# Redistributing a gather pass's rows over VectorE's stages, and the gate stage ahead of the output product, in a two-block transformer on one core

## The reference, cut to what matters

```python
def peer_ffn(x, w_q, sub_keys, u, v):      # 8 heads, top-16 of 16384 experts each: 128 rows per token
    ...
    expert_idx = jnp.take_along_axis(cand_i, top_pos, axis=-1)
    gates = jax.nn.softmax(top_s, axis=-1)
    ub = jnp.take(u, eb, axis=0)
    act = jax.nn.gelu(jnp.einsum('thkd,td->thk', ub, xb), approximate=False)
    vb = jnp.take(v, eb, axis=0)
    return jnp.einsum('thk,thkd->td', gb * act, vb)

# first_block, end of a layer: x = x + sigmoid(x @ ple_w_gate[i]) * (p[i] @ ple_w_proj[i])
# second_block: h = rms_norm_2(x); z = h @ w_in
#   x = x + concatenate([y_nsa, y_conv, y_gla]) @ w_out
#   x = x + (silu(h @ ffn_w_gate) * (h @ ffn_w_up)) @ ffn_w_down
```

## Time and profile before

| | us |
|---|---|
| median of 3 runs | 2252.76 |
| lowest, highest | 2241.89, 2260.28 |
| span of the profiled execution | 2259.6 |
| VectorE, TensorE, POOL busy in it | 1450.5, 1527.2, 985.0 |
| DMA, mean over the span | 337 GB/s |

### The profile page before, as it was taken

One profiled execution on the slowest core, in us unless ns is written; L12 is line 12 of the kernel. 1 busy time (PEld: TensorE's weight loads), 2 busy tenths in 40 slices (PEclk: granted clock), 3 DMA queues, 4 the chain that ended last, 5 costly groups with the idle time before them and its releaser, 6 DMA issues. The chain is left out here.

```text
span 2259.6 us, 17114 instructions
## 1 busy us (share of the span) xinstructions
PE 1527.2 (68%) x5282; PEld 879.4 (39%) x5282; DVE 1450.5 (64%) x3168; ACT 323.1 (14%) x778; POOL 985.0 (44%) x1058
## 2 busy tenths in 40 slices
PE   8987600467656539776573897666576656899998
PEld 7446600222225225422341552235252232376453
DVE  1236898779587875678688468786978676444101
ACT  1220100011112111111120111111321000123111
POOL 0102466667665555566455456653446444000000
PEclk9989855688867669987766899778767877899999
DMA  7436999999999999999999999999989999973672
GB/s 260 85 117 245 394 408 409 337 360 370 371 379 403 404 406 358 361 365 367 407 399 405 365 342 368 375 401 386 391 293 403 399 398 399 366 243 130 242 260 93
DMA packets 268005, 760.62 MB, mean 337 GB/s; under 512 B 21295, under 2 KB 46590, under 8 KB 267275
## 3 DMA queue, kind: packets, MB, share of 16 engines
q0 software_dynamic: 147456, 536.94, 61.8%
q1 hardware_dynamic: 120458, 222.60, 27.8%
HBM read 756.84 MB, written 2.62 MB: 336 GB/s over the span
## 5 line engine op out<-in xcount | busy, mean ns | idle before, releaser
L946 POOL DMA_INDIRECT ROWS<-in_peer_u,IDX x512 | 483.3, 944 | 455.5 <-DVE ROWS L991 266.9
L946 POOL DMA_INDIRECT ROWS<-in_peer_v,IDX x512 | 487.8, 953 | 357.2 <-PE bank L292 121.4
L991 DVE SCALAR_TENSOR_TENSOR ROWS<-ROWS,XP 128x1024 f32<-128x1024 f32 x512 | 602.3, 1215 | 23.7 <-issue 12.3
L995 DVE SCALAR_TENSOR_TENSOR XP<-ROWS,GATE,XP 128x1024 f32<-128x1024 f32 x316 | 405.8, 1284 | 155.9 <-DMA ROWS<-in_peer_v,IDX 133.7
L292 PE MATMUL bank<-ROWS,DG 128*128 128x512 f32 x774 | 380.0, 649 | 94.2 <-DMA ROWS<-in_peer_v,IDX 78.5
L292 PE MATMUL bank<-ring,XT 128*128 128x512 f32 (+6 forms) x912 | 392.7, 589 | 62.3 <-DMA ring<-in_ffn_w_up 32.0
L292 PEld LDWEIGHTS bank<-ring,XT 128*128 128x128 f32 x912 | 185.6, 214 | 249.9 <-issue 179.4
L292 PEld LDWEIGHTS bank<-ROWS,DG 128*128 128x128 f32 x774 | 157.5, 209 | 309.8 <-issue 201.8
L292 PE MATMUL bank<-XT,ring 128*128 128x128 f32 (+2 forms) x1504 | 209.4, 301 | 57.1 <-issue 27.4
L292 PEld LDWEIGHTS bank<-XT,ring 128*128 128x128 f32 (+1 forms) x1504 | 198.3, 204 | 71.8 <-issue 35.7
L307 PE MATMUL bank<-CN,X 128*128 128x128 f32 x128 | 27.1, 384 | 184.9 <-issue 90.7
(11 more groups left out here) (408 smaller groups left out, 1461.6 us busy)
## 6 DMA issues: line engine op xcount, KB each, us to landing
ring<-in_peer_w_q SPq DMA_DIRECT2D x16, 2048.0 KB
ring<-in_ple_w_gate SPq DMA_DIRECT2D x9, 2048.0 KB
ring<-in_ffn_w_gate SPq DMA_DIRECT2D x8, 2048.0 KB
ring<-in_ffn_w_up SPq DMA_DIRECT2D x7, 2048.0 KB
ring<-in_a_w_in SPq DMA_DIRECT2D x6, 2048.0 KB
ring<-in_w_in SPq DMA_DIRECT2D x6, 2048.0 KB
ring<-in_ffn_w_down SPq DMA_DIRECT2D x6, 2048.0 KB
ROWS<-in_peer_u,IDX POOLq DMA_INDIRECT x512
```

Source lines behind the costliest of these rows:

```text
L946: G.indirect_dma_start(ROWBUF[slot(n, c)][:, :], None, tables[table], bass.IndirectOffsetOnAxis(IDX[:, tt, c:c + 1], axis=0)).then_inc(row ...
L991: V.scalar_tensor_tensor(row, row, 1.0, XP[:, :], ALU.mult, ALU.mult, accum_out=ACTV[:, tt, c:c + 1]).then_inc(row_used, 1)
L995: V.scalar_tensor_tensor(XP[:, :], row, gate, XP[:, :], ALU.mult, ALU.add).then_inc(row_used, 1)
```

## The change

It moves rows of pass 6 between VectorE's stages and swaps two phases. No instruction's operands change.

```diff
 weigh:            -assert left >= 8
                   +assert left >= 4
 embed:            -gather_some(4)
                   +gather_some(9 if which == 1 and cb == 0 else 4)
 tails:                 phase(nsa_attention, tt, QT, NG, kept)
                   -phase(mixers_out, tt)
                    if tt == 0:
                        phase(weigh, 6)
                   +phase(mixers_out, tt)
                    phase(ffn, (tt,), with_pool=by_pool(tt))
 mixers_in:         take_turn(V, "xt", XT, xt_split(tt)[1])
                   -gather_some(10)
                   +gather_some(15)
                    ... the compression's blocks ...
                   -gather_some(8)
                   +gather_some(17)
                    V.wait_ge(bank_ready("conv"), turn("conv"))
                    ...
                    conv_steps(0, 16)
                   -gather_some(3)
                   +gather_some(4)
                    V.wait_ge(bank_ready("la"), turn("la"))
 nsa_attention:     for i in range(NH + 2):
                   -    gather_some(2)
                   +    gather_some(1)
```

More of the change, by code:

```diff
@@ L1074, in _ @@
                 left = rows_left()
-                assert left >= 8
+                assert left >= 4
                 V.wait_ge(*nth("gate_exp", 1))
@@ L1480, in _ @@
                         s = slice(cb * 512, cb * 512 + 512)
-                        gather_some(4)
+                        gather_some(9 if which == 1 and cb == 0 else 4)
                         V.wait_ge(bank_free(f"g{cb}{tt}"), turn(f"g{cb}{tt}"))
@@ L1913, in tails @@
                         phase(nsa_attention, tt, QT, NG, kept)
-                    phase(mixers_out, tt)
                     if tt == 0:
                         phase(weigh, 6)
+                    phase(mixers_out, tt)
                     phase(ffn, (tt,), with_pool=by_pool(tt))
@@ L2209, in _ @@
                 take_turn(V, "xt", XT, xt_split(tt)[1])
-                gather_some(10)
+                gather_some(15)
                 V.wait_ge(bank_free("ck"), turn("ck"))
@@ L2223, in _ @@
                         gather_some(1)
-                gather_some(8)
+                gather_some(17)
                 V.wait_ge(bank_ready("conv"), turn("conv"))
@@ L2250, in _ @@
                 conv_steps(0, 16)
-                gather_some(3)
+                gather_some(4)
                 V.wait_ge(bank_ready("la"), turn("la"))
@@ L2504, in _ @@
                 for i in range(NH + 2):
-                    gather_some(2)
+                    gather_some(1)
                     if i < NH:
```

## The result

The changed kernel takes 2269.86 us in the median of 6 runs (2265.64 to 2274.24), the kernel before 2256.51 in the median of 6 on the same chip: a ratio of 1.007, 95% interval 1.0049 to 1.0091. The forecast was 2 us slower; it is 13 us slower, outside the likeliest case (2248 to 2262) and inside the range of the rival called "weights come last". The profiled execution spans 2272.5 us against 2259.6.

What follows compares the result with a forecast made beforehand. Up to 1940 us DMA was taken to bound: bytes at 400 GB/s plus idle time. Counting idle DMA gave -1.6 us, counting weights +3.4; nearer the second, +2 us was taken: median 2255 us, range 2238 to 2270.

Steps and rivals of the forecast that it cites:

- likeliest case: Whole kernel: about 2 us slower, median 2255 us, within 2248 to 2262; chance 0.50.
- weights come last: Rival, feed-forward: weights never make up their 11 us late start; +11 to +16 us, 2266 us; chance 0.22.
- weights count: End of tile 0: weights and rows share DMA by packets; last product ends at 1941.4 against 1937.9 us, +3.4 us.
- Rows ahead of the waits: Embedding and mixers: 20 more rows fit VectorE's waits by time but must have landed; convolution input about 15 us later.
- Start of attention, +14.5: End of mixers: 11 rows not yet landed, at 1.29 us each while DMA is full, delay attention by 14.5 us.
- Attention, -3.5: Attention with ten rows fewer: TensorE binds, period 3.8 to 3.9 us, 35.1 us in place of 38.6.
- Gate stage 13.0, loads of the ring: Gate stage ahead of output product: 13.0 us instead of 15.3; the feed-forward's two early weight loads leave 24.0 us later.
- Idle DMA, 14 us for 15.6: Attention to first released weight buffer: idle 6.3, 0 and 6.5 us, with 1 for the clock about 14; -1.6 us.
- The feed-forward's end, 6.3 us of shrinkage: Feed-forward of tile 0, eight fewer rows left: starts 9.7 us later but ends only 3.4 us later.
- What follows tile 0, put at nothing: After about 1940 us, tile 1's serial work: nothing of this change is left there.
- Its point of decision: End of tile 0: the late-weights rival holds if the last down slice lands over 8 us after the last row.
- a fast tail makes up for a late start: End of tile 0: rows end at 1930 us, then the remaining 0.95 slot of weights takes 5 us alone, not 14.

Runs made afterwards that it cites:

- s3: Changed kernel with ScalarE's square root for the convolution's norm ahead of its wait for the compression's second half; 2198.03 us, ratio 1.0018 to the kernel before.
- k1: Changed kernel, unchanged, run on another chip than the first pair; 2201.14 us, ratio 1.0032 to the kernel before.
- f2: Changed kernel with ScalarE's root first and 14 v rows for 15 ahead of each feed-forward up product; 2199.13 us, ratio 1.0025 to the kernel before.
- g1: Changed kernel with ScalarE's root first and 12 v rows a feed-forward step for 15; 2190.05 us, ratio 0.9984 to the kernel before.
- s4: Changed kernel with tile 0's first-layer compression weights read in another row order, in long contiguous pieces; 2206.03 us, ratio 1.0050 to the kernel before.
- k0: Kernel before, unchanged, run on another chip than the first pair; 2194.46 us, ratio 1.0000.
- s1: Kernel before with only the gate stage and output product exchanged, early rows as before; 2197.16 us, ratio 1.0016 to the kernel before.
- f4: Kernel before with 14 v rows a feed-forward step for 15; 2194.12 us, ratio 1.0002 to the kernel before.
- g2: Changed kernel with 12 v rows a feed-forward step for 15, nothing else; 2196.30 us, ratio 1.0013 to the kernel before.
- f3: Changed kernel without the eight v rows in tile 0's output product, left over for the feed-forward; 2205.46 us, ratio 1.0059 to the kernel before.
- g3: Kernel before with ScalarE's root first, nothing else; 2189.07 us, ratio 0.9981 to the kernel before.

## Why the prediction was wrong

By products' ends on the first chip, tile 0 ended 15.7 us later (1937.89 to 1953.55), and what follows took 2.8 us less (321.7 to 318.9): 12.9 us. The forecast had +3.4 by its weights count. The difference of 12.3 us goes by its steps:

- **Rows ahead of the waits: the right kind, 15 us foreseen for the convolution.** Input +18.6 us, of which 1.65 lie ahead of the stretch: 16.9. VectorE's waits for `in_peer_u` stand where forecast.
- **Start of attention, +14.5: the step that failed most.** It was 26.6, 25.0 without those 1.65: 10.5 us too little. It was sized by landed rows alone. From the input to attention VectorE took 73.8 us instead of 65.8, and 6.7 of those 8.0 are as much as the root wait grew: ScalarE's root is queued behind its wait for the compression's second half, whose weight came late behind the rows. The prediction named the slip of the compression's packets only in a rival, and no wait behind it. With the root first the stretch lost 7.0 us (s3 against k1, two chips) and 4.3 and 4.0 us (f2, g1, each with its pair on one chip). Its own working has a slip too: 11 rows at 1.29 us are 14.2 us, not 14.5.
- **Attention, -3.5: right.** Period 3.77 us (forecast 3.8 to 3.9), first to last head -3.4 us, the clock at 0.50 in both.
- **Gate stage 13.0, loads of the ring.** TensorE's gap was 13.82 us. `ffu00` left 57.5 us after the start of attention (1715.37 - 1657.83) against 50.3 before; 59.8 was forecast: 2.3 better. The feed-forward started 19.1 us later, 7.5 less than attention where 4.8 was forecast: 2.7 better.
- **Idle DMA, 14 us for 15.6: wrong in direction.** It was 22 in those stretches and 4 at the end. The count had 10 rows and up to 12 buffers to refill in attention, 22 rows, and nothing idle in the gate stage. From 1657.83 to 1689.30 us the row queue moved 5.95 MB, 11 rows: with attention late and one row a head the buffers were full, and from 1657.8 to 1715 us GpSimd stood 27.6 us for VectorE's use of u rows. The gate stage had 267 GB/s.
- **The feed-forward's end, 6.3 us of shrinkage: mis-sized.** It shrank by 3.4 us, from its first transpose to the second load of an up slice (13.6 to 10.1 us), and then by nothing: 220.0 us both times. The weights keep their share whatever rows are left, so the eight fewer rows only ended earlier. The count expected a faster end from 1930 us, but rows were queued to 1939.7 us. It also took 7.5 us for that end (1932.5 + 11 + 5.4 = 1948.9 against its 1941.4), where there was little to take: from the start of the slice before last to the end TensorE needed 16.5 us before and 13.7 after, 2.7 less. That slice came 18.4 us later, 2.8 more than the second up load (15.6), so that even this was lost.

- **What follows tile 0, put at nothing.** "After it nothing of this change is left": it took 2.8 us less. No run isolates why.

Sum of the steps up to the end of tile 0: 1.65 + 10.5 - 2.7 + 2.9 = 12.3 us. The forecast then took 2 instead of the count's 3.4, leaning to the count by idle DMA, which had the wrong sign. The rival "weights come last" had it: 11 us late stays late, plus the mixers' slip, +11 to +16. Its point of decision, the last down slice over 8 us behind the last row, is not quite what came: TensorE waited for the slice before it to about the last row's time (1939.82 and 1939.70 us), had 13.7 us of work for the two, and ended 12.6 us behind the row. What the prediction took as a reason against the rival, that a fast tail makes up for a late start, fails since TensorE needs 13.7 us for the last two slices, however fast they come. At tile 0's end it has its +15.7 us, the top of its range; the 2.8 us behind tile 0 that bring the time to 13 are no part of it.

The Trainium skill's page "DMA: Bandwidth & Descriptors", section "Queues, rings and completion order", says that queues take turns packet by packet. The traces here agree wherever both queues had work waiting (713:711 in k1, 848:853 in the changed kernel, 304:293 in s4), and the forecast should have let it carry the weights' end.

On the chip of k0 and k1 the same change cost 7 us. Attention came 16.8 us later there, near the forecast's 14.5, but k0 was held up; against s1 and f4 it is 21 us, so the step fails there too. Why the first chip loses more is not settled; its longer root wait (8.84 to 5.41 us) may be a part of it.

## What to carry to other kernels

In these traces, while two DMA queues are both backlogged, the bytes of each go by its packets' size over the sum (2 KB beside 4 KB: 1.42 and 2.59 MB in 10 us), and work taken out of one does not speed the other until it runs empty: look for which of the two ends last, and leave that queue room. A wait of an engine is not free space by itself: follow what is queued behind the waiting instruction on the other engines, and count the waits up to the next common point as one. A stage moved ahead delays the release of the buffers behind it, even if it moves no byte: here the second up slice, and with it the end, moved back.

## What the runs showed of the hardware

Packets of two backlogged queues were served one for one with 1, 2 and 13.5 KB beside 4 KB. The same kernel took 2256.5 us on one chip and 2193.0 to 2194.2 on four others; in 450 to 550 us of the kernel before DMA moved 364 GB/s on the first and 409 on the one of k0_before, though both move 398 to 399 in 300 to 400 us of the changed stretch. What follows tile 0 took 318.9 us in nine traces, 320.6 in g1 and g2, 321.7 to 326.5 where the last row was used at or behind the products' end (the kernel before, k0, f3, f4), and 323.1 to 324.9 in s1, f2 and g3, whose granted clock, a mean over its two levels of 1.2 and 2.4 GHz, was 0.91 instead of 1.00 over 40 us of the same stage:
```profile
1896.80:1936.80 40.00, 39.08 (x200) 27.73 (x199) 7.96 (x16) 6.94 (x17) 0.57 (x1) 0.91 0.61 204
```
```profile
1900.30:1940.30 40.00, 39.07 (x222) 27.81 (x221) 7.95 (x16) 7.86 (x21) 0.57 (x1) 1.00 0.68 227
```
(s1_swap_only, then k1_after; the clock is the column before the DMA share.) Those three profiled executions took 2203.45, 2202.40 and 2194.13 us where their kernels' medians are 2197.16, 2199.13 and 2189.07, so some of the spread of 10 us between runs of one kernel may be this; what lowered the clock was not looked for.
